# Ones products on the matmul engine around the first transposes, and the first weights taken in quarters and halves

## The reference

```python
def rms_norm(x, g):
    y = xf * lax.rsqrt(jnp.mean(xf * xf, axis=-1, keepdims=True) + RMS_EPS)
    return (y * g).astype(x.dtype)
# first_block: p = rms_norm(x, norm_mix_pre) @ w_in      (1024 x IN_COLS)
# rwkv7_time_mix, on p's RWKV columns:
p = p + (token_shift(p) - p) * mu
w_raw = (w0 + jnp.tanh(xw) @ w_up)      # xw, xa, xg: the last 256 RWKV columns
a = jax.nn.sigmoid((a0 + xa @ a_up))
g = jax.nn.sigmoid(xg) @ g_up
```

## Time and profile before

| | |
|---|---|
| median of 3 runs | 944.87 us (942.68 to 945.28) |
| the profiled execution | 942.33 us, span of the instructions 940.2 us |
| PE busy | 914.4 us, 97% of the span |
| DVE, ACT, POOL busy | 559.5, 405.7, 35.9 us |
| mean granted PE clock | 0.982 |
| DMA | 140.61 MB, 149 GB/s over the span |

### The profile page before, as it was taken

How to read it: one execution, slowest core, us unless ns; L and a number is a source line. 1 busy time by engine, 2 the same in 40 slices (tenths; PEclk the granted TensorE clock), 3 DMA queues, 4 the chain that set the end, 5 groups by cost and what they waited for, 6 DMA issues and landing times.

```text
span 940.2 us, 14880 instructions
## 1 busy us (share of the span) xinstructions
PE 914.4 (97%) x6336; PEld 842.3 (90%) x6336; DVE 559.5 (60%) x638; ACT 405.7 (43%) x495; POOL 35.9 (4%) x39
## 2 busy tenths in 40 slices
PE   6999999999999999999999999999998999999997
PEld 6999889898989899999999898998897889999996
DVE  5898555626315876555555665548574485565564
ACT  6453444431112764343334644455553453344332
POOL 0000000615100000000000000000000000000000
PEclk9999999999859999999999999999999999999999
DMA  9646433200004736556555464443551446556541
GB/s 321 215 145 209 128 107 125 90 2 1 1 1 169 255 120 201 192 165 219 178 174 187 132 223 139 141 143 144 196 179 46 135 160 198 184 196 198 182 134 45
DMA packets 96708, 140.61 MB, mean 150 GB/s; under 512 B 2448, under 2 KB 79376, under 8 KB 96656
## 3 DMA queue, kind: packets, MB, share of 16 engines
q1 hardware_dynamic: 96368, 139.72, 45.1%
q10 hardware_dynamic: 288, 0.13, 0.0%
HBM read 138.79 MB, written 1.05 MB: 149 GB/s over the span
## 4 chain that ended last, share of the span: by engine, by line
PE 92%; issue 3%; ACT 2%; DVE 2%; DMA 1%; POOL 0%; SPq 0%; DVEq 0%; ACTq 0%; POOLq 0%
PE PS L388 91%; ACT xh L953 1%; DVE wlo L1347 1%; PE PS L463 1%; DMA raw<-in_w_in_dram 1%; ACT whi L953 1%; ACT junk L953 0%; DVE xl L1377 0%; PE PS L791 0%; POOL Xm L939 0%; PE PS L539 0%; DVE xn L1839 0%; PE PS L635 0%; ACT mp L953 0%; DVE small L1784 0%
## 5 line engine op out<-in xcount | busy, mean ns | idle before, releaser
L1347 DVE TENSOR_TENSOR wlo<-raw,whi 128x2048 fp32r<-128x2048 f32 x125 | 285.9, 2292 | 144.7 <-ACT whi L953 144.7
L388 PE MATMUL PS<-xh,whi 128*128 128x256 f32 x1136 | 325.0, 286 | 8.7 <-DVE xl L1377 8.0
L388 PE MATMUL PS<-xh,wlo 128*128 128x256 f32 x1136 | 322.1, 283 | 0.0
L388 PE MATMUL PS<-xl,whi 128*128 128x256 f32 x1136 | 322.0, 283 | 0.0
L953 ACT ACTIVATE whi<-raw 128x2048 fp32r<-128x2048 f32 (+1 forms) x127 | 240.2, 1895 | 175.4 <-PE PS L388 161.2
L388 PEld LDWEIGHTS PS<-xh,whi 128*128 128x128 f32 x1136 | 218.4, 192 | 15.2 <-issue 8.4
L388 PEld LDWEIGHTS PS<-xl,whi 128*128 128x128 f32 x1136 | 218.6, 192 | 1.0
L388 PEld LDWEIGHTS PS<-xh,wlo 128*128 128x128 f32 x1136 | 218.5, 192 | 0.0
L388 PE MATMUL PS<-whi,fh 128*128 128x512 f32 x216 | 84.3, 391 | 0.0
L388 PE MATMUL PS<-wlo,fh 128*128 128x512 f32 x216 | 84.3, 390 | 0.0
L388 PE MATMUL PS<-whi,fl 128*128 128x512 f32 x216 | 84.0, 389 | 0.0
(11 more groups left out here) (298 smaller groups left out, 1248.2 us busy)
## 6 DMA issues: line engine op xcount, KB each, us to landing
raw<-in_w_in_dram SPq DMA_DIRECT2D x32, 1024.0 KB, 5.4
raw<-in_w_up_dram SPq DMA_DIRECT2D x16, 1024.0 KB, 5.5
raw<-in_w_down_dram SPq DMA_DIRECT2D x16, 1024.0 KB, 5.0
raw<-in_w_ffn_gate_dram SPq DMA_DIRECT2D x11, 1024.0 KB, 5.3
raw<-in_w_ffn_up_dram SPq DMA_DIRECT2D x11, 1024.0 KB, 5.3
raw<-in_w_ffn_down_dram SPq DMA_DIRECT2D x11, 1024.0 KB, 4.9
raw<-in_w_kv_mem_dram SPq DMA_DIRECT2D x8, 1024.0 KB, 5.4
raw<-in_w_o_dram SPq DMA_DIRECT2D x4, 1024.0 KB, 8.3
```

Source lines behind the costliest of these rows:

```text
L388: return nc.tensor.matmul(o, l, r, start=start, stop=stop, **kw)
L1347: V.tensor_tensor(wlo[u % RING][:], raw[u % RING][:], whi[u % RING][:].bitcast(f32), ALU.subtract) \
```

## The change

Four things change, all in the first 40 us.

- PE gets `turn_over(n)`: n float32 products of the tile `one` with itself into bank 3, whose result nobody reads. Nine stand ahead of the transposes, behind a wait for the memset of `one`, and six stand behind them.
- Unit 0 is loaded, rounded, split and used in quarters of 512 columns (two k each), unit 1 is rounded, split and used in halves (four k each). ACT and DVE now do two blocks of x, then one quarter; both halves of unit 1 come ahead of the squares. For these two units `by_feature` runs k outside and f inside.
- `scale_row` moves from behind unit 0 to behind unit 1.
- The outputs of the seven RWKV units rotate through banks 0, 1 and 3, so the wait for `out_evac` starts at i = 3.

```diff
+        RW_BANK = [(0, 1, 3)[i % 3] for i in range(len(U_RW))]
+        EARLY = {0: UNIT // 4, 1: UNIT // 2}
...
-                    sp.dma_start(raw[0][:, 0:UNIT // 2].rearrange("p (k n) -> p k n", n=width), src[:, 0:KD // 2]).then_inc(sem("half_loaded"), 16)
-                    sp.dma_start(raw[0][:, UNIT // 2:].rearrange("p (k n) -> p k n", n=width), src[:, KD // 2:]).then_inc(raw_loaded[0], 16)
+                    for q in range(4):
+                        sp.dma_start(raw[0][:, q * EARLY[0]:(q + 1) * EARLY[0]].rearrange("p (k n) -> p k n", n=width),
+                                     src[:, 2 * q:2 * q + 2]).then_inc(sem(f"quarter{q}_loaded") if q < 3 else raw_loaded[0], 16)
...
+                if u in EARLY:
+                    for k in range(kt):
+                        if k * n % EARLY[u] == 0:
+                            part = k * n // EARLY[u] + 1
+                            if part * EARLY[u] < UNIT:
+                                pe.wait_ge(sem(f"part_split{u}"), part)
+                            else:
+                                pe.wait_ge(sem("unit_split"), u + 1)
...
+            def turn_over(n):
+                for _ in range(n):
+                    mm(PS[:, 3 * 512:3 * 512 + P], one[:], one[:], True, True)
+            pe.wait_ge(sem("ones_set"), 1)
+            turn_over(9)
             pe.wait_ge(sem("ident_loaded"), 16)
             transpose_in("n1", xres, 4, lambda t, c: pe.wait_ge(sem(f"x_loaded{t}"), 16))
+            turn_over(6)
             for i, u in enumerate(U_RW):
-                if i >= 2:
-                    pe.wait_ge(sem("out_evac"), i - 1)
-                by_feature(u, xh, xl, i % 2, None if i else "n1")
-                if i == 0:
-                    pe.wait_ge(sem("ones_set"), 1)
+                if i >= 3:
+                    pe.wait_ge(sem("out_evac"), i - 2)
+                by_feature(u, xh, xl, RW_BANK[i], None if i else "n1")
+                if i == 1:
                     scale_row("n1", 2)
...
+            for q in range(4):
+                round_T("n1", "norm_mix_pre", xh, 0, range(2 * q, 2 * q + 2), 4)
+                act.wait_ge(sem(f"quarter{q}_loaded") if q < 3 else raw_loaded[0], 16)
+                hi_part(0, q)
+            act.wait_ge(raw_loaded[1], 16)
+            for q in range(2):
+                hi_part(1, q)
             for t in range(NT):
                 act.wait_ge(sem(f"x_loaded{t}"), 16)
                 squares("n1", xres[:, t, :], t)
             root("n1")
-            for u in range(1, RING):
+            for u in range(2, RING):
                 hi(u)
...
+            for q in range(4):
+                rest_T("n1", "norm_mix_pre", xh, xl, 0, range(2 * q, 2 * q + 2), 4)
+                lo_part(0, q)
+            for q in range(2):
+                lo_part(1, q)
             inverse("n1")
```

More of the change, by code:

```diff
@@ L394, in split @@
             def split(u, n, later=0):
-                if u:
+                if u not in EARLY:
                     pe.wait_ge(sem("unit_split"), u + 1 + later)
-                else:
-                    pe.wait_ge(sem("half_split"), 1)
                 return (whi[u % RING][:].rearrange("p (k n) -> p k n", n=n),
@@ L407, in by_feature @@
                 wh, wl = split(u, n, later)
+                if u in EARLY:
[6 more added lines that the diff above has]
+                                pe.wait_ge(sem("unit_split"), u + 1)
+                        if st:
+                            pe.wait_ge(norm_sem(st, "xT"), nth(st, "xT", max(k + 1, 2)))
+                        for f in range(n // P):
+                            o = PS[:, b * 512 + f * SEQ:b * 512 + (f + 1) * SEQ]
+                            fs = slice(f * P, (f + 1) * P)
+                            mm(o, wh[:, k, fs], hi[:, k, :], k == 0 and f == 0, False, skip_group_check=True)
+                            mm(o, wh[:, k, fs], lo[:, k, :], False, False, skip_group_check=True)
+                            last = mm(o, wl[:, k, fs], hi[:, k, :], False, k == kt - 1, skip_group_check=True)
+                    last.then_inc(sem("units_used"), 1)
+                    return
                 for f in range(n // P):
@@ L413, in by_feature @@
                             pe.wait_ge(norm_sem(st, "xT"), nth(st, "xT", max(k + 1, 2)))
-                            if u == 0 and k == kt // 2:
-                                pe.wait_ge(sem("unit_split"), 1)
                         fs = slice(f * P, (f + 1) * P)
@@ L1031, in _, with hi_part @@
             act.wait_ge(sem("eps_set"), 1)
-            act.wait_ge(sem("half_loaded"), 16)
-            A_(whi[0][:, 0:UNIT // 2], raw[0][:, 0:UNIT // 2], ACT.Copy).then_inc(sem("half_hi"), 1)
             act.wait_ge(sem("par_loaded"), 16)
[L1035 to L1038, removed]
+            def hi_part(u, q):
+                w = EARLY[u]
+                whole = (q + 1) * w == UNIT
+                A_(whi[u][:, q * w:(q + 1) * w], raw[u][:, q * w:(q + 1) * w], ACT.Copy) \
+                    .then_inc(sem("hi_done" if whole else f"part_hi{u}"), 1)
+            for q in range(4):
[5 more added lines that the diff above has]
+                hi_part(1, q)
             for t in range(NT):
@@ L1384, in _, with lo_part @@
             dve.wait_ge(sem("par_loaded"), 16)
[L1385 to L1389, removed]
+            def lo_part(u, q):
+                w = EARLY[u]
+                whole = (q + 1) * w == UNIT
+                p_ = slice(q * w, (q + 1) * w)
+                dve.wait_ge(sem("hi_done" if whole else f"part_hi{u}"), u + 1 if whole else q + 1)
+                V.tensor_tensor(wlo[u][:, p_], raw[u][:, p_], whi[u][:, p_].bitcast(f32), ALU.subtract) \
+                    .then_inc(sem("unit_split" if whole else f"part_split{u}"), 1)
+            for q in range(4):
[3 more added lines that the diff above has]
+                lo_part(1, q)
             inverse("n1")
@@ L1401, in _ @@
                     dve.wait_ge(sem("mixed"), i)
-                V.tensor_tensor(s[:, :, 1:SEQ + 1], two(i % 2), spread(rs1[:]), ALU.mult).then_inc(sem("out_evac"), 1)
+                V.tensor_tensor(s[:, :, 1:SEQ + 1], two(RW_BANK[i]), spread(rs1[:]), ALU.mult).then_inc(sem("out_evac"), 1)
                 dve.wait_ge(sem("out_evac"), i + 1)
```

## The result

The changed kernel takes 947.33 us (median of 8 runs, 945.91 to 948.32), the kernel before in the same comparison 943.75 (8 runs, 942.6 to 945.28). The ratio is 1.0036 with a 95% interval of 1.0024 to 1.0049: **slower by 0.36%, 3.6 us**, where I forecast no change. The profiled execution took 948.23 us with a span of 946.2. (`by_feature` stands at L403 of the listing, not at the L373 that the text above gives.)

What follows compares the result with a forecast made beforehand. PE was taken as the bound, busy 914.4 of 940.2 us; -1.0 (slack at the LoRA wait), +0.1 (queue) and +1.0 (clock) gave +0.1 us, so a median of 945.0 us, range 941.8 to 946.9.

Steps and rivals of the forecast that it cites:

- the gate: PE's LoRA products wait for `lora_in`, behind unit 4's landing and rounding; ready at 30.3 us, leaving 1.0 us of slack.
- The start: Transposes through unit 2 on PE: earlier unit 0 and full clock put PE 4.3 us early at unit 2's end.
- The landing of unit 4: DMA queue stays full, so unit 4 still lands at 27.7 us; +0.1 us taken, 0 to 0.7 upwards.
- The clock: PE's clock falls behind the new 3.4 us stand before the LoRA products: 1.0 us lost, bounds 0 and 1.5.
- Sum: Whole kernel: -1.0 slack at the LoRA wait, +0.1 queue, +1.0 clock, giving +0.1 us.
- The clock isn't woken: Rival: ones products do nothing or transposes start at half clock; PE stands 1.6 us, result 944.3 us; chance 0.12.
- The landing moves forward: Rival: instruction packet no longer holds up unit 4, which lands at 26.3 us; about 943.0 us; chance 0.12.
- No gate at all: Rival: nothing holds PE at the LoRA products, the full 4.3 us reaches the end, 940.6 us; chance 0.07.
- The rival on the slower side: A second instruction packet lands ahead of unit 4; landing 1.0 us later decides; 1.7 slower, 946.6 us; chance 0.09.
- the forecast's own case: PE stands from 26.9 to 30.3 us before the LoRA products; median 945.0 us; chance 0.60.
- Slower: Verdict that the whole kernel measures slower, beyond the 0.3% (2.8 us) bound: chance some 0.06.
- The rule of the Trainium skill: Long DMA wait between matmuls halves PE's clock: loss the whole 1.5 us, sum 0.6 slower; without it, 0.9 faster.

Runs made afterwards that it cites:

- e1: Changed kernel with tanh and sigmoid on ACT ahead of the rounding of unit 4: 939.68 us, ratio to before 0.9953.
- e2: Kernel before with only tanh and sigmoid moved ahead of the rounding of unit 4: 943.60 us, ratio to before 0.9998.
- e7: Changed kernel with tanh and sigmoid ahead of unit 4's rounding, and the norm-factor spread products over 128 rows in place of 8: 926.18 us.
- e10: Changed kernel with spread products over 128 rows and 14 more ones products on PE ahead of the LoRA wait: 928.88 us.
- e9: Changed kernel with the norm-factor spread products over 128 rows in place of 8, LoRA wait as it was: 932.10 us.
- e3: Changed kernel with 14 more ones products on PE ahead of its wait for the LoRA input: 943.38 us, ratio to before 1.0013.
- e5: Changed kernel without its 15 products of ones; quarters, halves and moved scale row stay: 944.39 us, ratio to before 0.9997.
- e4: Changed kernel with both LoRA products over all 128 rows in place of 64 each: 944.91 us, ratio to before 1.0009.
- e11: Changed kernel with spread products over 128 rows and both LoRA products over all 128 rows: 933.46 us, ratio to before 0.9890.
- e6: Kernel before with only the 9 and 6 products of ones added: 944.03 us, ratio to before 0.9994.
- e8: Kernel before with only the norm-factor spread products over 128 rows in place of 8: 929.80 us, ratio to before 0.9850.

## Why the prediction was wrong

- **What bounds the kernel, and the gate.** Right, and the main step. I read from ACT's 4.95 us behind a DMA that `lora_in` holds PE at 30.3; PE stood for 3.29 us there (forecast 3.4) and went on at 31.12 (forecast 30.3). That the stand came out so close is luck: both its ends came 0.8 to 0.9 us later than forecast. e1 shows that it is this wait, e2 that PE was the later one before.
- **The start.** Near. Unit 0 from 9.85 (forecast 9.0), the split of unit 0 done at 13.95 (13.1), the end of unit 2 near 27.8 (26.9): all 0.85 late. 0.65 of it is the first transposed pair, ready at 7.35 rather than 6.7, since PE ran at half pace up to 7 us. So PE was 3.4 us early there and not 4.3. Behind the gate this counted only through the DMA queue, which is the next point.
- **The landing of unit 4.** Mis-sized, and by the wrong path: +0.1 taken, bounds 0 to 0.7; the rounding started 0.8 later (28.55 against 27.72). I had the queue full up to `msk`. It ran thin from 14 to 16 us, and `msk` landed 2.2 us later; the instruction packet moved out of the way, which I had put at 0, and unit 4 followed `msk` 1.4 us sooner. That the two nearly cancel was luck. So the gain at the LoRA products was 0.2 us and not 0.9.
- **The clock: the term that failed.** I took 1.0 us from bounds of 0 and 1.5. The upper bound came from the rows of 11.2 to 14.6 us and of 721.2 to 724.6, both of which show 0.50 for 3.4 us, and I took that for the whole extent of a fall. The same trace had a fall of 24 us, from 253.6, visible in two digits of the earlier trace rows (8 and 5) that I left unread. It has another cause, as e7 shows, but it would have told me that 3.4 us was no bound. Measured: 10.2 us at 0.50 and 4.6 us lost in the profiled execution. e10 (3.2 us back, same chip as e9) isolates it, and e3 (4.0 us back, medians from different comparisons) agrees.
- **Sum:** -0.2 + 4.6 = +4.4 where I had +0.1. The remaining 1.6 between the profiles is the stretch at 71.8 us. The medians differ by 3.6.
- **Rivals.** "The clock isn't woken" has its answer in e5: 944.39 where I said 944.3, a stand of 1.75 where I said 1.6, and no fall. The match of the time is partly chance: it had a gain of 1.0 us at the LoRA products, and they start at 31.55, 0.2 later than before. "The landing moves forward" named something that did happen, the packet out of the way, but `msk` came later by more. "No gate at all" is refuted by the stand of 3.29 us. The rival on the slower side had its threshold in a later landing by 1.0 us and a price of 1.7. The landing was late by 0.8, and it needed no threshold: the forecast's own case was the slow one. "Slower" had 0.06 because every case was priced with at most 1.5 us for the clock.
- **The rule of the Trainium skill** (page TensorE: Matmul & The Clock Gate, section Loop structure matters more than you think) that a long wait between matmuls puts PE back at half clock: the trace agrees, 0.50 behind a stand of 3.29 us. I put 0.6 us slower to it, with the same wrong bound. But I wrote that both old falls agree with it, and the one at 721.2 us doesn't: PE's stands ahead of it are 0.79, 0.75 and 1.68 us, with products in between. e9 has the same three stands (0.79, 0.75, 1.69) 9 us earlier and no fall.

## What to carry to other kernels

Speed at the head of a program is worth only what the next wait lets through. Look for engines that wait for something which doesn't move with the engine that was made faster, even if the chain doesn't name them, and move the small step in front of the large one on that engine (tanh ahead of the rounding). A new stand of PE has two prices, the time and the clock behind it: let the upper bound of the second cover the longest fall that the trace shows, not only the nearest. In the profile, read every digit of the clock's row first; what stood behind two low digits in the middle was, with the short stretch near 70 us, worth 14.6 us, four times what the change cost. At the head of a span check the clock against the pace of the matmuls.

## What the runs showed of the hardware

- A stand of 3.3 to 3.4 us put PE's clock to 0.50 in the changed kernel, in e4 and in e9, for 10.2, 6.8 and 6.8 us, and one of 2.9 us in the kernel before (8.3 to 11.2 us) and in e11, for 3.4 us each. Stands of 1.75 (e5) and 1.1 us (e6) did not. That gives no threshold: in the kernel before the clock also fell at 721.2 us, behind stands of 0.79, 0.75 and 1.68 us close together, and in e9 it didn't behind the same three. Products of a tile with itself, whose result nobody reads, kept the clock at 1.00 over the same time (e3, e10).
- Products over 8 rows let the clock fall though PE had no gap (69.6 us after; 251 us before). The same products over 128 rows, 120 of them zero, took the same time and left the clock at 1.00: 14.6 us by medians in the kernel before (944.38 to 929.80). One execution of the kernel before in a later comparison took 930.6 us with a mean clock of 0.998, so it can also escape the fall, as one run of e5 did (933.56 us, 0.996); in its other runs beside the experiments the mean clock was 0.978 to 0.984.
- A DMA of 1 MB landed 4.4 us behind the transfer ahead of it with an instruction packet in between (4.2 in e2 and e8), and 3.0 us behind it where the packet had passed earlier (after; 3.0 to 3.1 in e1, e3, e4, e5, e6, e9).
